# First range of a fused decoder block: one k tile of the modulation on TensorE, main loads behind the modulation weights, two splits ahead of the modulation

## What is computed

```python
c_act = jax.nn.silu(c)
mod = c_act @ ada_w[l] + ada_b[l]                    # (1, 2048) x (2048, 12288)
sh1, sc1, g1, sh2, sc2, g2 = [m[:, None, :] for m in jnp.split(mod, 6, axis=-1)]
u = rms_norm(x, mix_norm_pre[l]) * (1.0 + sc1) + sh1 # the modulation, first half
y = token_mixer(u, w_in[l], ret_w_o[l], moba_w_o[l], w_out[l])
...
proj = u @ w_in                                      # (256, 2048) x (2048, 16384)
```

## Time and profile before

| | us |
|---|---|
| median of 3 runs | 1862.79 (1861.95 to 1862.82) |
| the profiled execution's own time | 1866.73 |
| its span in the profile | 1864.7 |
| VectorE busy | 1332.4 (71%) |
| ScalarE busy | 869.8 (47%) |
| GpSimd busy | 190.0 (10%) |

### The profile page before, as it was taken

How to read it: one execution, slowest core, us unless ns; L and a number is a source line. 1 busy time by engine, 2 the same in 40 slices (tenths; PEclk the granted TensorE clock), 3 DMA queues, 4 the chain that set the end, 5 groups by cost and what they waited for, 6 DMA issues and landing times.

```text
span 1864.7 us, 25986 instructions
## 1 busy us (share of the span) xinstructions
PE 1823.6 (98%) x8980; PEld 1546.9 (83%) x8980; DVE 1332.4 (71%) x1896; ACT 869.8 (47%) x1005; POOL 190.0 (10%) x269
## 2 busy tenths in 40 slices
PE   5999999999999999999999989999999999999998
PEld 5888888888888888888888868888888888888886
DVE  4788687878777777778887566777677777755555
ACT  4533454445454545454444546444444444544444
POOL 0000022222222222222220000000000000000000
PEclk8999999999999999999999999999999999999999
DMA  9999688878878787868885644655555556555553
GB/s 352 386 332 333 191 263 259 279 245 262 269 245 273 242 277 240 276 226 293 286 272 185 232 158 137 199 183 188 195 180 194 189 182 197 184 199 185 202 185 108
DMA packets 249842, 432.69 MB, mean 232 GB/s; under 512 B 12356, under 2 KB 103156, under 8 KB 249136
## 3 DMA queue, kind: packets, MB, share of 16 engines
q1 hardware_dynamic: 227936, 360.77, 58.7%
q0 software_dynamic: 20736, 67.34, 10.5%
q10 hardware_dynamic: 1104, 3.70, 0.5%
HBM read 429.66 MB, written 2.10 MB: 232 GB/s over the span
## 4 chain that ended last, share of the span: by engine, by line
PE 95%; DVE 2%; DMA 1%; ACT 1%; SPq 0%; issue 0%; DVEq 0%; ACTq 0%
PE ps L866 17%; PE ps L540 16%; PE ps L542 15%; PE ps L541 15%; PE ps L874 9%; PE ps L931 4%; PE ps L933 4%; PE ps L932 4%; PE ps L562 1%; PE ps L656 1%; PE ps L658 1%; PE ps L657 1%; DMA ada_first<-in_ada_w 1%; PE ps L605 1%; DVE ada_acc L1415 1%; DVE w_low L1341 1%
## 5 line engine op out<-in xcount | busy, mean ns | idle before, releaser
L1341 DVE TENSOR_TENSOR w_low<-stage,w_high 128x1024 fp32r<-128x1024 f32 x608 | 743.9, 1224 | 439.8 <-ACT w_high L977 420.7
L977 ACT ACTIVATE w_high<-stage 128x1024 fp32r<-128x1024 f32 x552 | 584.0, 1060 | 769.4 <-PE ps L542 399.3
L540 PE MATMUL ps<-w_high,lhs 128*128 128x512 f32 x1280 | 507.2, 396 | 0.0
L542 PE MATMUL ps<-w_high,lhs 128*128 128x512 f32 x1280 | 500.5, 391 | 0.0
L541 PE MATMUL ps<-w_low,lhs 128*128 128x512 f32 x1280 | 499.9, 391 | 0.0
L866 PE MATMUL ps<-lhs,w_high 128*128 128x512 f32 x1408 | 338.4, 392 | 2.6 <-issue 2.6
L866 PEld LDWEIGHTS ps<-lhs,w_high 128*128 128x128 f32 x1408 | 259.6, 189 | 53.1 <-issue 2.8
L542 PEld LDWEIGHTS ps<-w_high,lhs 128*128 128x128 f32 x1280 | 241.1, 188 | 51.3
L541 PEld LDWEIGHTS ps<-w_low,lhs 128*128 128x128 f32 x1280 | 241.5, 189 | 48.7
L540 PEld LDWEIGHTS ps<-w_high,lhs 128*128 128x128 f32 x1280 | 241.6, 189 | 48.5
L524 POOL DMA_DIRECT2D ada_ring<-in_ada_w x256 | 185.4, 724 | 785.2 <-DVE ada_acc L1367 534.0
(11 more groups left out here) (194 smaller groups left out, 1180.2 us busy)
## 6 DMA issues: line engine op xcount, KB each, us to landing
stage<-in_w_in SPq DMA_DIRECT2D x100, 1024.0 KB, 6.4
stage<-in_ffn_w_up SPq DMA_DIRECT2D x176, 512.0 KB, 4.3
ada_ring<-in_ada_w POOLq DMA_DIRECT2D x256, 256.0 KB, 5.4
stage<-in_ffn_w_down SPq DMA_DIRECT2D x44, 1024.0 KB, 5.0
ada_first<-in_ada_w SPq DMA_DIRECT2D x64, 512.0 KB, 7.6
stage<-in_w_in SPq DMA_DIRECT2D x56, 512.0 KB, 7.5
stage<-in_ret_w_o SPq DMA_DIRECT2D x16, 1024.0 KB, 7.0
stage<-in_moba_w_o SPq DMA_DIRECT2D x16, 1024.0 KB, 6.9
```

Of the source, the lines that this page charges most:

```text
L540: pe.matmul(acc, hi, w_high[:, slot, k, :], start=kt == 0, stop=False)
L542: last = pe.matmul(acc, lo, w_high[:, slot, k, :], start=False, stop=kt == KT - 1)
L977: act.activation(w_high[:, h % 4, :, :], stage[:, slot, 2 * (h % 2):2 * (h % 2) + 2, :], ACT.Copy).then_inc(high_ready, 1)
L1341: dve.tensor_tensor(w_low[:, h % 4, :, :], stage[:, slot, 2 * (h % 2):2 * (h % 2) + 2, :], w_high[:, h % 4, :, :].bitcast(F32), ALU.subtra ...
```

## The change

It changes range 0 in four ways and the later ranges in one.

- In range 0 only the very last k tile (row 15, the second row of slot 7) goes to TensorE (`direct_row`, 8 products); VectorE takes the other 15. Slot 7 is then released by both.
- SyncE issues all eight slots of range 0 ahead of main load 0.
- TensorE issues 40 warming products ahead of the direct row, 4 between it and the sum, and 10 behind the sum.
- High parts 0 and 1 stand ahead of the modulation on ScalarE; on VectorE split 1 stands behind shift and scale, and ahead of the `lhs` parts.
- In the later ranges the 16 direct products are cut into 8, 6 and 2 instead of 4, 6 and 6.

```diff
         def ada_steps(st):
-            return KT - ada_rows(st)
+            return KT - (ada_rows(st) if st else 1)
         def direct_slot(st):
-            return ada_slots(st) - 2
+            return ada_slots(st) - 2 if st else ada_slots(st)
...
         def steps_through(st, slot):
-            return ada_steps_before(st) + ada_rows(st) * (slot + 1 if slot < direct_slot(st) else slot)
+            rows = ada_rows(st) * (slot + 1 if slot < direct_slot(st) else slot)
+            return ada_steps_before(st) + min(rows, ada_steps(st))
...
                         sp.wait_ge(ada1_step, steps_through(st_, slot_))
+                        if st_ == 0 and slot_ == ada_slots(0) - 1:
+                            sp.wait_ge(ada1_direct, 1)
...
-            for slot in range(2):
+            for slot in range(ada_slots(0)):
                 first_ada(0, slot)
...
                         first_load(n, st, pair, g)
-                        if n == 0:
-                            for slot in range(2, ada_slots(0)):
-                                first_ada(0, slot)
...
+            def direct_row():
+
+                q, width = ada_slots(0) - 1, 4 * len(FIRST_PAIRS[0])
+                pe.wait_ge(ada1_in[q % 4], 32 * (q // 4 + 1))
+                for i in range(width):
+                    at = (ada_rows(0) - 1) * width + i
+                    last = pe.matmul(ps[:, 7, i:i + 1], ada_first[:, q % 4, at * P:(at + 1) * P], c_act[:, KT - 1:KT],
+                                     start=i == 0, stop=False)
+                last.then_inc(ada1_direct, 1)
...
                         if g == SUM_BEHIND[st] and (i, k) != (0, 0):
-                            direct_sums(st + 1, (None, 0, 4, 10)[2 * i + k], (None, 4, 10, 16)[2 * i + k])
+                            direct_sums(st + 1, (None, 0, 8, 14)[2 * i + k], (None, 8, 14, 16)[2 * i + k])
...
-            keep_warm(16)
-            direct_sums(0, 0, 16)
+            keep_warm(40)
+            direct_row()
+            keep_warm(4)
             sum_first(0)
-            keep_warm(14)
+            keep_warm(10)
...
             for n in range(8 * G_FIRST):
-                if prepares_before(n) is not None:
+                if n == 2:
+                    first_u(0)
+                elif n != 1 and prepares_before(n) is not None:
                     first_u(prepares_before(n))
...
+                    if st == 0:
+                        low_part(n, n // 2 % 4, n)
                     for pair in FIRST_PAIRS[st]:
                         lhs_pair(0, pair, src_b)
                 add_streamed(n)
-                low_part(n, n // 2 % 4, n)
+                if st != 0:
+                    low_part(n, n // 2 % 4, n)
```

## The result

The change made the kernel slower: 1872.67 us at the median of 4 executions (1865.18 to 1874.56) against 1862.54 for the kernel before, a ratio of 1.0037 [1.0022 to 1.0052]. The three times known ahead of the prediction, 1861.95 to 1862.82, are as low as the lowest 7 of these 32; whether that was chance or another chip is not known. In the later series the kernel before has medians of 1864.4 to 1866.2, and the change costs some 5 to 6 us and widens the spread from 6 to 11 us.

A forecast was written before the change was run, and what follows sets the result against it. TensorE, busy for 98% of the span, was taken as the bound. From the median of 1862.8 us, start -3.8 and later sums -2.2 gave 1856.8 us, with a range of 1851.5 to 1861.2.

The forecast's parts named there:

- The rival on the slower side: Three later sums: clock also falls behind the new runs of 16, twice per range, costing 14.4 us; 1872; chance 0.04.
- the early fall: Start: clock falls at 33.7 in the direct row; start gains only 1.8 us, later sums nothing; 1861.0; chance 0.22.
- the later sums: Column sums of the three later ranges: fewer clock falls with cut 8, 6, 2, worth -2.2 us (0 to -3.2).
- For 20 I take one in five, at 1.6: Later sums: clock falls behind one in five last runs of 20 narrow records, 1.6 us each; 1.0 us for three sums.
- the first run grows from 8 to 16: Later sums: first direct piece grows to 16 narrow records; no cost in the main forecast.
- The start: Range 0: first useful product at 43.4 instead of 47.73, less 0.5 us at half clock: -3.8 us (-1.8 to -7.2).
- VectorE's 15 rows: Range 0: VectorE takes 15 rows in one stretch, last done at 35.0; the added 1.34 us is paid from removed waits.
- The moved load brings slots 1.36 us earlier: Start: main load 0 behind slot 7 lets slots 2 to 7 land 1.36 us earlier, slot 7 at 33.15.
- slot 7 comes no earlier: Start rival: queue runs dry or transfers are slower, direct row starts at 34.5, gain 0.9 to 1.4 less; 1858.0; chance 0.10.
- The clock falls at 35.8, behind the direct row: Start: direct row ends at 34.8 at full rate; clock falls at 35.8, sum runs at half rate to 39.2.
- The second split costs nothing: Start, VectorE: split 1 (1.22 us) ahead of lhs subtraction lies in a 1.82 us wait for ScalarE; costed at nothing.
- The transfers of the next range hold an earlier start at 6.6 us: Next range: its last slot lands at 73.8 regardless of TensorE's start, so a shift over 6.6 us is lost again.

The follow-up runs named there:

- i1: Changed kernel with cut 8, 6, 2 in range 0 only, 6, 6, 4 in ranges 1 and 2: 1862.53 us, ratio 0.9990 to the kernel before.
- e3: Changed kernel without any edit, timed and profiled again: 1871.49 us, ratio 1.0027 to the kernel before.
- e1: Changed kernel with the later sums cut 4, 6, 6 again: 1864.59 us, ratio 0.9996 to the kernel before.
- i2: Changed kernel with cut 6, 6, 4 in range 0 and 8, 6, 2 in ranges 1 and 2: 1872.42 us, ratio 1.0038.
- e2: Kernel before with only the later sums cut 8, 6, 2: 1868.57 us, ratio 1.0025 to the kernel before.
- h4: Kernel before with only main load 0 moved behind all eight slots: 1862.83 us, ratio 0.9992 to the kernel before.
- f5: Changed kernel with later ranges' narrow products spread, two behind each of 12 triples of wide products: 1897.18 us, ratio 1.0175 to the kernel before.
- e4: Changed kernel with later ranges' narrow products spread, four behind each of six triples of wide products: 1870.80 us, ratio 1.0028 to the kernel before.
- h2: Changed kernel with cut 6, 6, 4 and 50 warming products instead of 40 ahead of the direct row: 1860.86 us, ratio 0.9984.

## Why the prediction was wrong

**Direction and size.** 1856.8 was forecast, faster with 0.74. It came out slower, outside the range. The rival on the slower side named the kind of event (falls behind the new runs of 16) and almost the time (1872), and was given 0.04. Its time is in part luck: it had the falls at all three sums, and i1 shows no loss from the first of them. (The upper end of the range, 1861.2, is given as the early fall, whose own sum is 1861.0; this changes nothing.)

**The step that failed** is the later sums, forecast at -2.2 us. The cut 8, 6, 2 against 4, 6, 6 in the same kernel costs 5.8 us by the ratios and 6.9 at the medians (e3 and e1). "For 20 I take one in five, at 1.6" was sound: in the profiles the clock fell behind 1 of 10 last runs of 20 records. But in the sentence next to it, "the first run grows from 8 to 16" was priced at nothing, apart from the rival. i2 and i1, one series, differ by 9.9 us, and a first piece of 16 records in ranges 1 and 2 (12 in i1) carries it. The rows of before showed no run of 16 in the first place, and the absence of falls behind runs of 8 and 12 was read as if it bounded 16. A fall was also priced by the ones seen, 1.6 to 3.2 us. That fits the two falls in the changed kernel's profile (3.2 and 1.6), which is of its fastest execution. Where the clock did not come back within the mixed work, one fall cost 6.4 us (i2, range 1) to 8.0 us (e2).

**The start.** Forecast -3.8, measured -1.6 in the profile; e1 is 1 us lower at the median, and its interval, 0.9986 to 1.0005, does not exclude nothing. *VectorE's 15 rows*: right but for 0.65 us of waiting at slot 7. *The moved load brings slots 1.36 us earlier*: right by itself (h4, 33.14), but undone in the change, by the instruction fetch as far as the landings show. This is the rival "slot 7 comes no earlier", though by another cause than it named. *The clock falls at 35.8, behind the direct row*: it fell in it, at about 35.1, between the forecast and the early rival. In the twelve profiles with the changed kernel's start it fell anywhere from 33.5 to 36.9, and the first wide product came at 44.5 to 47.7 (two profiles with the start of before, the kernel before and e2: 47.73 and 46.84), so one profile can't tell the cases apart. *The Trainium skill in the early rival*: page "TensorE: Matmul & The Clock Gate", section "HAM oscillation — how this bites in real kernels", is about waits for transfers that are longer than the bursts of products before them. Here the wait was 2.31 us behind 9.13 us of warming products, so the section bears on that rival less than the prediction took it to. *The second split costs nothing*: right. *The transfers of the next range hold an earlier start at 6.6 us*: no row disproves it, and the start never came near.

**The base.** The prediction took the profiled execution as 3.9 us worse than usual. In 32 executions the median was 1865.57, and 10 of them took 1866.73 or more. So it was 1.2 us above the median, and the reason for lowering the gain at the later sums from 3.8 to 2.2 was weaker than it looked.

## What to carry to other kernels

Between wide products, narrow ones can cost more than their own time once the clock has fallen, for a mix of both can hold it down (6.8 us in the changed kernel, 17.1 in e2, 27.3 in f5): price a fall by what stands between it and the next stretch of purely wide work, not only by the falls already in the trace. Don't give the largest share of narrow work to the piece that stands behind a wait (in the profiles with three pieces it held behind up to 12 records, behind 16 not always), but don't push it all to the end either: 2, 6, 8 was 5 us slower than 6, 6, 4. And before a critical transfer, look at the instructions as well: they are fetched over the same DMA engines, and a fetch can delay what filler products are meant to bridge.

## What was not expected of the hardware

The same mix of three wide products and four narrow records ran at full rate for 13 us (f5, 75.5 to 89) and at half rate for 27 us (f5, 125.8 to 153.1), and in both cases it had begun at that rate. A fetch of 16 KB of instructions on one DMA engine went with a delay of 1.3 us of a transfer of 512 KB spread over 16 engines. And the kernel before, unchanged, spreads over 6 us between executions on one chip, where i1 keeps within 2.1. Two things that differ between profiles fit this: where the clock falls at the later sums (84.9 and 180.5 in the kernel before, 84.0 and 131.7 in e1, with the same cut), and a stretch at half rate that begins between 1104 and 1140 us in every profile, where TensorE waits (5.0 us at most in the kernel before) and no edit was made, and which lasts 10.2 us in most and 17.1 us in e4, f5, h2 and i2.
